# Norm entries of a two-layer-type transformer begun inside the program that feeds them; last chunks by token tile, scaled rows turned by the identity, GpSimd's first low halves

## The reference

```python
for l in range(2):                                  # first block
    h = rms_norm(x, attn_norm[l])
    x = x + mix(h @ w_in[l]) @ w_out[l]             # attentions and a gated scan in mix
    hf = rms_norm(x, ffn_norm[l]) @ w_up[l]
    x = x + (gelu(conv(gate(hf))) * val(hf)) @ w_down[l]          # w_down: 2816 x 1024
for l in range(2):                                  # second block
    y = mix2(x @ w_in_2[l])
    h = layer_norm(ALPHA * x + y @ w_out_2[l], ln1_g[l], ln1_b[l])
    x = layer_norm(ALPHA * h + peer_ffn(h, ...), ln2_g[l], ln2_b[l])
```

## Time and profile before

| | us |
|---|---|
| median of 3 runs | 2827.97 (2822.35 to 2829.43) |
| the profiled execution | 2826.24 |
| its span | 2824.5 |
| TensorE busy (matmuls) | 2651.6, 94% |
| VectorE, ScalarE, GpSimd busy | 2054.0, 1496.3, 176.2 |
| mean granted clock of TensorE | 0.979 |

### The profile page before, as it was taken

One profiled execution on the slowest core, in us unless ns is written; L12 is line 12 of the kernel. 1 busy time (PEld: TensorE's weight loads), 2 busy tenths in 40 slices (PEclk: granted clock), 3 DMA queues, 4 the chain that ended last, 5 costly groups with the idle time before them and its releaser, 6 DMA issues. The chain is left out here.

```text
span 2824.5 us, 56598 instructions
## 1 busy us (share of the span) xinstructions
PE 2651.6 (94%) x17272; PEld 2387.2 (85%) x17272; DVE 2054.0 (73%) x4610; ACT 1496.3 (53%) x2949; POOL 176.2 (6%) x136
## 2 busy tenths in 40 slices
PE   7989999989988899799999999988998999999997
PEld 6869988779977899799988888777998999888886
DVE  5767767767767668877767777787589777677777
ACT  5545556645555444466655555555454566555554
POOL 0000000000000044300000000000344000000000
PEclk9989999989999999999999999999999999999999
DMA  5225654236653477555567777625576555677775
GB/s 194 86 68 166 186 154 162 74 112 184 186 162 101 150 222 225 165 171 176 174 199 233 234 233 232 213 92 174 174 230 192 160 175 171 187 233 235 232 234 179
DMA packets 194306, 503.49 MB, mean 178 GB/s; under 512 B 22561, under 2 KB 88353, under 8 KB 192801
## 3 DMA queue, kind: packets, MB, share of 16 engines
q1 hardware_dynamic: 194208, 502.28, 56.8%
HBM read 467.59 MB, written 34.60 MB: 178 GB/s over the span
## 5 line engine op out<-in xcount | busy, mean ns | idle before, releaser
L182 DVE TENSOR_TENSOR w_lo<-w_raw,w_hi 128x512 fp32r<-128x512 f32 (+1 forms) x1464 | 994.8, 684 | 357.3 <-ACT w_hi L173 337.4
L173 ACT ACTIVATE w_hi<-w_raw 128x512 fp32r<-128x512 f32 (+2 forms) x1592 | 925.7, 621 | 203.4 <-PE banks_right L217 136.7
L215 PE MATMUL up_up<-hT_hi,w_hi 128*128 128x256 f32 x2048 | 595.8, 291 | 26.6 <-DVE w_lo L182 20.5
L217 PE MATMUL up_up<-hT_hi,w_lo 128*128 128x256 f32 x2048 | 582.6, 284 | 0.0
L216 PE MATMUL up_up<-hT_lo,w_hi 128*128 128x256 f32 x2048 | 582.3, 284 | 0.0
L215 PEld LDWEIGHTS up_up<-hT_hi,w_hi 128*128 128x128 f32 x2048 | 396.1, 193 | 31.2 <-DVE w_lo L182 23.9
L227 PE MATMUL banks_left<-w_hi,expert_hi 128*128 128x512 f32 x1024 | 408.1, 399 | 7.8 <-DVE w_lo L182 7.8
L228 PE MATMUL banks_left<-w_lo,expert_hi 128*128 128x512 f32 x1024 | 407.6, 398 | 0.0
L229 PE MATMUL banks_left<-w_hi,expert_lo 128*128 128x512 f32 x1024 | 407.4, 398 | 0.0
L216 PEld LDWEIGHTS up_up<-hT_lo,w_hi 128*128 128x128 f32 x2048 | 395.6, 193 | 0.0
L217 PEld LDWEIGHTS up_up<-hT_hi,w_lo 128*128 128x128 f32 x2048 | 395.0, 193 | 0.0
(11 more groups left out here) (374 smaller groups left out, 3863.6 us busy)
## 6 DMA issues: line engine op xcount, KB each, us to landing
w_raw<-in_peer_u_c SPq DMA_DIRECT2D x256, 512.0 KB, 3.5
w_raw<-in_peer_v SPq DMA_DIRECT2D x256, 512.0 KB, 3.6
w_raw<-in_w_up_c SPq DMA_DIRECT2D x88, 512.0 KB, 3.7
expert_gelu_held<-expert_gelu SPq DMA_DIRECT2D x256, 128.0 KB, 1.7
expert_back<-expert_gelu_held SPq DMA_DIRECT2D x256, 128.0 KB, 3.3
w_raw<-in_w_down SPq DMA_DIRECT2D x44, 512.0 KB, 4.1
w_raw<-in_w_in_r SPq DMA_DIRECT2D x40, 512.0 KB, 3.6
w_raw<-in_w_in_c SPq DMA_DIRECT2D x32, 512.0 KB, 4.0
```

The source lines that it names most:

```text
L173: self.nc.scalar.activation(self.w_hi[:, k % SLOTS, 0:width], self.raw_half(k, width), ACT.Copy).then_inc(self.sem("w_hi_done"), 1)
L182: self.nc.vector.tensor_tensor(self.w_lo[:, k % SLOTS, 0:width], self.raw_half(k, width), self.w_hi[:, k % SLOTS, 0:width].bitcast(F32), A ...
L215: self.nc.tensor.matmul(bank, hi, self.hT_hi[:, c, :], start=(c == 0), stop=False)
L217: last = self.nc.tensor.matmul(bank, lo, self.hT_hi[:, c, :], start=False, stop=(c == DC - 1))
```

## The change

It touches every entry, the end of every program that feeds one, and `finish`.

- The last chunk of an out-projection (the last two in `SecondMiddle` and `DownPhase`) goes by token tile first: `last_halves` finishes both banks of tile 0, then those of tile 1. It signals `acc_done` for the two banks of tile 0.
- The next entry exists before its block: in the feeding program VectorE adds three of the four quarters of the sum and, for a layer norm, takes their statistics and the scale of tile 0; ScalarE splits the first two weight halves, and squares tile 0 (RMS) or loads the square root's table and takes tile 0's root (layer norm).
- In the entry, RMS turns tile 0 by the diagonal matrix as before; tile 1 is scaled by rows, half on ScalarE, half on VectorE, and turned by the identity. A layer norm scales and shifts `x` in place and turns both tiles by the identity; `rows` then multiplies that by the gain.
- The first four low halves are made by GpSimd; high halves 2 and 3 stand between the copies of the chunks. TensorE waits for single chunks.
- In `finish` token tile 0 goes through GpSimd (times gain, plus bias, by halves), tile 1 through VectorE, and four stores of half the size go out.

```diff
+    def last_halves(self, pe, chunks, acc, done):
+        for t in range(TT):
+            cols = slice(t * P, (t + 1) * P)
+            for i, (k, act_hi, act_lo) in enumerate(chunks):
+                end = i == len(chunks) - 1
+                for h in range(2):
+                    if t == 0:
+                        pe.wait_ge(self.sem("w_lo_done"), k + h + 1)
+                    hi, lo = self.w_hi[:, (k + h) % SLOTS, :], self.w_lo[:, (k + h) % SLOTS, :]
+                    bank = acc[:, t, h, :]
+                    self.nc.tensor.matmul(bank, act_hi[:, cols], hi, start=False, stop=False)
+                    self.nc.tensor.matmul(bank, act_hi[:, cols], lo, start=False, stop=False)
+                    last = self.nc.tensor.matmul(bank, act_lo[:, cols], hi, start=False, stop=end)
+                    if t == TT - 1:
+                        last.then_inc(self.sem("w_used"), 1)
+                    elif end:
+                        last.then_inc(done, 1)
...
+    def arrived(self, dve, t, h):
+        if t == 0:
+            dve.wait_ge(self.acc_done, h + 1)
+        else:
+            dve.wait_ge(self.K.sem("w_used"), self.k0 - 1 + h)
+    def add_half(self, t, h):
+        x = self.x[:, t, h]
+        return self.K.nc.vector.tensor_tensor(x, x, self.add[:, t, h], ALU.add)
+    def early_vector(self, dve):
+        for t, h in ((0, 0), (0, 1), (1, 0)):
+            self.arrived(dve, t, h)
+            self.add_half(t, h).then_inc(self.added, 1)
+    def early_scalar(self, act, junk=None):
+        for h in range(2):
+            self.K.split_hi(act, self.k0 + h, self.width)
     def chunk_ready(self, pe, c):
-        if c % 2 == 0:
-            pe.wait_ge(self.lo_done, c // 2 + 1)
+        pe.wait_ge(self.lo_done, c + 1)
+    def pool(self, pool):
+        for h in range(EARLY):
+            self.K.split_lo_too(pool, self.k0 + h, self.width)
...
+class RmsEntry(TurnEntry):
+    def square(self, act, t, h, junk):
+        if self.add is not None:
+            act.wait_ge(self.added, 2 * t + h + 1)
+        self.K.nc.scalar.activation(junk, self.x[:, t, h], ACT.Square,
+                                    accum_out=self.K.ns[:, t, h:h + 1]).then_inc(self.squared, 1)
+    def sqrt(self, act, t):
+        act.wait_ge(self.squared, 2 * t + 2)
+        act.wait_ge(self.based, t + 1)
+        ns = self.K.ns[:, t]
+        self.K.nc.scalar.activation(ns[:, 3:4], ns[:, 1:2], ACT.Sqrt, scale=1.0 / D, bias=ns[:, 2:3]).then_inc(self.root, 1)
+    def base(self, dve, t):
+        dve.wait_ge(self.squared, 2 * t + 1)
+        ns = self.K.ns[:, t]
+        self.K.nc.vector.tensor_scalar(ns[:, 2:3], ns[:, 0:1], 1.0 / D, EPS1, ALU.mult, ALU.add).then_inc(self.based, 1)
+    def early_scalar(self, act, junk):
+        super().early_scalar(act)
+        for h in range(2):
+            self.square(act, 0, h, junk[:, h])
+    def tensor(self, pe):
+        pe.wait_ge(self.scaled, 1)
+        for c in range(DC):
+            self.K.nc.tensor.matmul(self.ps[:, c, 0:P], self.K.x[:, 0, c * P:(c + 1) * P], self.diag[:], start=True, stop=True)
+        for c in range(DC):
+            if c == 0:
+                pe.wait_ge(self.left_half, 1)
+            if c == DC // 2:
+                pe.wait_ge(self.right_half, 1)
+            self.turn(c, 1, self.rows)
+    def scalar(self, act):
+        K, A = self.K, self.K.nc.scalar
+        if self.add is None:
+            self.early_scalar(act, self.spare[:, 0])
+        self.sqrt(act, 0)
+        for h in range(2):
+            self.square(act, 1, h, self.spare[:, 0, h])
+        self.sqrt(act, 1)
+        act.wait_ge(self.scaled, 2)
+        A.activation(self.spare[:, 1, 0], self.x[:, 1, 0], ACT.Copy, scale=K.ns[:, 1, 4:5]).then_inc(self.left_half, 1)
+        K.split_hi(act, self.k0 + 2)
+        for j in range(DC // 2):
+            act.wait_ge(self.turned, j + 1)
+            for c in (2 * j, 2 * j + 1):
+                A.activation(K.hT_hi[:, c, :], self.ps[:, c, :], ACT.Copy, scale=self.gain[:, c:c + 1]).then_inc(self.hi_done, 1)
+            if j == 1:
+                K.split_hi(act, self.k0 + 3)
+    def vector(self, dve):
+        K, V = self.K, self.K.nc.vector
+        link = lambda ins: K.dve.link(dve, ins)
+        self.base(dve, 0)
+        if self.add is not None:
+            self.add_half(1, 1).then_inc(self.added, 1)
+        dve.wait_ge(self.root, 1)
+        link(V.reciprocal(K.ns[:, 0, 4:5], K.ns[:, 0, 3:4]))
+        V.tensor_scalar(self.diag[:], K.ident[:], K.ns[:, 0, 4:5], None, ALU.mult).then_inc(self.scaled, 1)
+        self.base(dve, 1)
+        dve.wait_ge(self.root, 2)
+        V.reciprocal(K.ns[:, 1, 4:5], K.ns[:, 1, 3:4]).then_inc(self.scaled, 1)
+        dve.wait_ge(self.scaled, 2)
+        V.tensor_scalar(self.spare[:, 1, 1], self.x[:, 1, 1], K.ns[:, 1, 4:5], None, ALU.mult).then_inc(self.right_half, 1)
+        for j in range(DC // 2):
+            dve.wait_ge(self.hi_done, 2 * j + 2)
+            for c in (2 * j, 2 * j + 1):
+                V.scalar_tensor_tensor(K.hT_lo[:, c, :], self.ps[:, c, :], self.gain[:, c:c + 1],
+                                       K.hT_hi[:, c, :].bitcast(F32), ALU.mult, ALU.subtract).then_inc(self.lo_done, 1)
...
+class LayerNormEntry(TurnEntry):
+    def norm_act(self, act, t, part):
+        act.wait_ge(self.ready, t + 1)
+        x, ns = self.K.x[:, t, part], self.K.ns[:, t]
+        self.K.nc.scalar.activation(x, x, ACT.Identity, scale=ns[:, 3:4], bias=ns[:, 4:5]).then_inc(self.rows_act, 1)
+    def early_vector(self, dve):
+        link = lambda ins: self.K.dve.link(dve, ins)
+        for h in range(2):
+            self.arrived(dve, 0, h)
+            link(self.add_half(0, h))
+            ins = self.stats(0, h)
+        link(ins)
+        self.variance(dve, 0)
+        self.arrived(dve, 1, 0)
+        link(self.add_half(1, 0))
+        self.K.dve.mark(self.stats(1, 0))
+        self.inverse(dve, 0)
+    def early_scalar(self, act, junk=None):
+        if self.gain is not None:
+            super().early_scalar(act)
+        self.K.nc.scalar.activation(self.K.ns[:, 0, 5:6], self.K.eps[:, 1:2], ACT.Sqrt)
+        self.sqrt(act, 0)
+    def last_stats(self, dve):
+        link = lambda ins: self.K.dve.link(dve, ins)
+        link(self.add_half(1, 1))
+        link(self.stats(1, 1))
+        self.variance(dve, 1)
+    def tensor(self, pe):
+        for t in range(TT):
+            for c in range(DC):
+                if c == 0:
+                    pe.wait_ge(self.rows_act, t + 1)
+                if t == 1 and c == DC // 2:
+                    pe.wait_ge(self.rows_dve, 1)
+                self.turn(c, t, self.K.x[:, t])
+    def scalar(self, act):
+        K, A = self.K, self.K.nc.scalar
+        self.norm_act(act, 0, slice(0, D))
+        self.sqrt(act, 1)
+        self.norm_act(act, 1, slice(0, D // 2))
+        for j in range(DC // 2):
+            two = slice(2 * j, 2 * j + 2)
             if j % 2 == 0:
                 act.wait_ge(self.turned, j + 1)
                 for c in (2 * j, 2 * j + 1):
                     A.activation(self.h[:, c, :], self.ps[:, c, :], ACT.Identity, scale=self.gain[:, c:c + 1],
                                  bias=self.bias[:, c:c + 1]).then_inc(self.shifted[0], 1)
             act.wait_ge(self.shifted[j % 2], 2 * (j // 2 + 1))
+            if j == 0:
+                for c in (0, 1):
+                    A.activation(K.hT_hi[:, c, :], self.h[:, c, :], ACT.Copy).then_inc(self.hi_done, 1)
+            else:
+                A.activation(K.hT_hi[:, two, :], self.h[:, two, :], ACT.Copy).then_inc(self.hi_done, 2)
+            if j < 2:
+                K.split_hi(act, self.k0 + 2 + j, self.width)
     def vector(self, dve):
         K, V = self.K, self.K.nc.vector
+        self.last_stats(dve)
+        self.inverse(dve, 1)
+        dve.wait_ge(self.ready, 2)
+        V.tensor_scalar(self.x[:, 1, 1], self.x[:, 1, 1], K.ns[:, 1, 3:4], K.ns[:, 1, 4:5], ALU.mult,
+                        ALU.add).then_inc(self.rows_dve, 1)
         def shift(j):
                 V.tensor_scalar(self.h[:, c, :], self.ps[:, c, :], self.gain[:, c:c + 1], self.bias[:, c:c + 1],
                                 ALU.mult, ALU.add).then_inc(self.shifted[1], 1)
+        def low(c, n):
+            dve.wait_ge(self.hi_done, c + n)
+            part = slice(c, c + n)
+            V.tensor_tensor(K.hT_lo[:, part, :], self.h[:, part, :], K.hT_hi[:, part, :].bitcast(F32),
+                            ALU.subtract).then_inc(self.lo_done, n)
+        shift(1)
+        low(0, 1)
+        low(1, 1)
+        low(2, 2)
+        shift(3)
+        low(4, 2)
+        low(6, 2)
...
+                if i == DC - 2 and h == 0:
+                    K.last_halves(pe, [(k0 + k + 2 * u, *self.out_parts(self.OUT_ORDER[i + u])) for u in range(2)],
+                                  acc, self.following.acc_done)
+                elif i < DC - 2:
...
     def tensor_tile(self, pe, j, n):
```

(17 more changed lines are left out.)

386 lines of the change are left out of this document (171 added, 215 removed).

## The result

The changed kernel took 2783.6 us in the median of 4 runs (2781.1 to 2789.9), the kernel before 2827.6 in 4 runs beside it: a ratio of 0.985 (95% interval 0.983 to 0.987), 44 us less. The forecast was 2817 and its range went down to 2808: the way was right, the size was not. The profiled span fell from 2824.5 to 2782.2 us, 42.3 us.

The account below looks back on a forecast made before the run. TensorE's work plus its waits was taken as the bound; 8.7 + 0.5 + 1.9 + 6.3 - 2.6 - 0.4 = 14.4 us, less 3.5 for the clock, gave 11: 2817 us, own range 2811 to 2822, wider 2808 to 2828.

Parts of the forecast that it names:

- the part on the bound: Opening step: TensorE, busy 94% of the span, bounds the kernel, with one chain of waits at each hand-over.
- 3.5 for the clock: Allowance for TensorE's clock falling to half at the norm hand-overs: 3.5 us lost, bounds 0 and 9.
- RMS entries: Three RMS norm entries with a sum: an earlier first tile gains 2.9 us each, 8.7 in all.
- First entry and turn: First RMS entry, with nothing to begin early, gains 0.5 us; the turn without a norm gains 1.9.
- Layer norms: Three layer-norm entries: first tile at E + 14.1 against 16.2 (E: last matmul's end), 2.1 us each, 6.3 in all.
- E + 14.5: Sign of error: a layer norm's first tile done later than 14.5 us after E, the last matmul's end.
- (a): Rival, nothing in the way: full clock, no turns with GpSimd; 18 us gained, 2810 us, chance 0.15.
- (b): Rival, given back: later waits absorb the entries' gain, half the 14 us or less, 2822 to 2828; 0.25 with (d).
- (c): Rival, colder and slower than before: clock at half in all seven hand-overs, 23 us cost, 2836 us, chance 0.10.
- The wait in `DownPhase`: One wait for tile 127's low halves before both last tiles costs 1.3 us in each DownPhase, 2.6 in all.
- The end: In finish, alternating VectorE and GpSimd gain 0.3 us, more clears cost 0.7: together -0.4, between -0.9 and +2.0.
- Rival (d): Early work does not start early, as VectorE or ScalarE are still busy: about 3 us gained, 2825; 0.25 with (b).

Follow-up runs that it names:

- e1: The kernel before with 160 bytes of unused SBUF allocated behind the epsilons and nothing else: 2804.6 us, ratio 0.992.
- e3: The kernel after the change with 32 unused bytes ahead of expert_hi and expert_lo alone: 2807.8 us, ratio 0.993.
- i1: The kernel after the change with DownPhase's last two tiles waited for separately and the RMS entries' root table loaded ahead of the squares: 2784.0 us.
- e5: The kernel after the change with nothing of a norm entry begun inside the program that feeds it: 2806.9 us, ratio 0.993.
- m1: A kernel of TensorE alone: 512-column fp32r products at varied starts of weights and moving rows, 227.0 to 234.3 ns from matmul to matmul.
- m2: As m1 with the moving rows fixed, only the weights' start moved, and the width varied: 113.3 to 120.1 ns at 256 columns.
- i3: i1's kernel with hT moved to start 64 bytes ahead of w_hi within 256 (192 unused bytes ahead, 64 behind): 2750.5 us, ratio 0.973.
- i4: i1's kernel with hT moved to start 64 bytes behind w_hi within 256 (64 unused bytes ahead, 192 behind): 2774.5 us, ratio 0.981.

## Why the prediction was wrong

**The step that failed** is the last sentence of the part on the bound: "Behind each first tile TensorE is the bound again, so I let a tile that is done earlier move all that follows", with a rate taken as fixed. The term for the steady loops was nothing, and the prediction gives no reason why their rate should stay. The change left the instructions of the down product's rounds as they were, but it moved their operands against each other: 234.3 ns from matmul to matmul became 226.7. e1 gives that part without the change and e3 takes it away from it, 23 to 24 us by the medians. Between the 11 us forecast and the 42.3 of the span lie 31.3: 22.8 in the two down products (-20.2 where +2.6 stood), 4.7 in the mixing programs, 1.1 in the feed-forward's outputs and 2.7 at the hand-overs (16.2 where 17.0 less 3.5 for the clock stood). The allocation of `ns` and `nstats` stood in the diff, and so did the two rates in the trace of before, 0.227 us in the out-projection and 0.234 in the down product. I used the first in the sum and did not ask why the second was longer. By the map the answer lay in the starts: `hT_hi` and `w_hi` are alike within 256 bytes, `expert_hi` and `w_hi` were 96 apart.

**RMS entries.** 8.7 us forecast, 8.3 measured, unevenly: 3.4 and 3.3 where I wrote 2.9, and 1.6 in the one between. There the table load stood where I had put it and TensorE turned 1.7 us sooner, as in the others, but the clock was at half:

```profile
400.94 1.28 ACT L392 ACT_TABLE_LOAD   x1 [0.92 <-DVE norm_scalars L398]
...
403.12 3.78 PE L408 MATMUL banks_right<-norm_scale,x 128*128 128x128 f32 x16 [3.20 <-DVE norm_scale L442]
```

The same sixteen rows took 2.05 us in the first feed-forward's entry, so the lower clock has the 1.7 us that are missing. i1 gains 1.5 us by moving the load of 1.28 away, and its sixteen rows took 3.42 us, partly at full clock. First entry and turn: 0.4 and 2.2 against 0.5 and 1.9.

**Layer norms.** 6.3 forecast and 4.7 measured. In the first one E is 899.28. Its low beside GpSimd took 1.35 us, where others took 0.69, as forecast, and the first product came at E + 8.3 instead of E + 12.2; but the first tile was done at E + 15.3, later than the E + 14.5 that I had named as a sign of error:

```profile
899.05 0.39 PE L255 MATMUL banks_right<-w_hi,hT_lo 128*128 128x512 f32 x1
...
907.59 0.55 PE L224 MATMUL banks_right<-hT_hi,w_hi 128*128 128x256 f32 x1 [0.83 <-DVE hT_lo L573]
...
908.43 1.35 DVE L573 TENSOR_TENSOR hT_lo<-ln_chunks,hT_hi 128x512 fp32r<-128x512 f32 x1 [0.66 <-ACT hT_hi L550]
...
914.55 0.63 ACT L182 ACTIVATE w_hi<-w_raw 128x512 fp32r<-128x512 f32 x1 [2.34 <-PE banks_right L226]
```

The 24 products took 7.0 us, before 4.0 (928.28 to 932.23). The stretches of 20 us, after and then before (busy share and count of each engine, then the granted clock):

```profile
903.00:923.00 20.00, 17.19 (x111) 16.03 (x110) 11.53 (x21) 10.91 (x20) 3.76 (x3) 0.74 0.62 213
```
```profile
915.00:935.00 20.00, 13.36 (x87) 12.27 (x86) 15.11 (x29) 11.10 (x19) 0.00 (x0) 0.83 0.41 160
```

A mean of 0.74 is 10.4 us at half clock (1.2 of 2.4 GHz), 0.83 is 6.8, and now they lie on the products, where before most fell on turning and waiting. That gives back 3.0 of the 3.9 us. So the clock cost about what I had feared in the first and last layer norm (1.1 and 1.0 us under the sum at full clock, 1.0 feared in each) and 1.7 in one RMS entry, and nothing to be seen in the others: hand-overs and waits together came to -13.9 us, between the 14.4 at full clock and the forecast's 11. The 4.5 us that the prediction names for the clock are 5.0 by its own figures (three layer norms at 1.0, four RMS entries at 0.5).

**The rivals (a) to (c).** (a), nothing in the way, is refuted as a mechanism, by the clock of 0.5 and the low of 1.35 us; its 18 us are 4 above the 13.9, and its 1.7 for the end should have been 2.6 by the prediction's own E + 8.8. (b), given back, does not hold: all 16.2 us are still there at a matmul well behind the first tiles, and the mixing programs behind them got no longer but by 0.2 us in one. (c) is refuted: no hand-over got slower. The turn's stretch held no time at half clock in any of the 14 kernels, with sixteen turns between its products.

**The wait in `DownPhase`** was 1.13 us twice (1.3 forecast), the release as computed. That the pair need not wait as one (i1) gives back 0.5, not all.

**The end.** 0.74 us shorter, where 0.4 longer was forecast. The clears were last and are longer as forecast (47 in 3.3 us, before 36 in 2.5), but the work ahead of them ended at E + 9.7 (E = 2767.70) and not at E + 11.4: the four operations of VectorE took 1.5 to 1.75 us each beside GpSimd's of 1.3 to 1.7, largely at the same time and not in strict turns. The last of each:

```profile
2775.29 1.59 POOL L3158 TENSOR_TENSOR x<-x,w_raw 128x512 f32<-128x512 f32 x1
2775.68 1.75 DVE L3176 SCALAR_TENSOR_TENSOR x<-x,norm_scalars,w_raw 128x512 f32<-128x512 f32 x1
```

**The mixing programs.** -4.7 us, of which 3.4 in one: it had 13.7 us at half clock before and 3.4 after. No term of the forecast spoke of the clock outside the hand-overs. That gain need not be the change's: the same program took 104.9 us with 3.4 at half clock in e2 too, which is the kernel before with 32 unused bytes.

**Rival (d):** e5 shows the contrary of (d): the early work began early, and 23 us hang on it. That is more than the 16 that the hand-overs gained, since without the early start the new order is worse than the old one in the layer norms and at the end.

## What to carry on

Before you take a steady loop as fixed, list which buffers the diff moves; a cadence that shifts by some ns with equal waits is the sign. Compare the start-to-start time of equal matmuls between phases: a difference within one trace may be a gain that lies open. Hold the starts of weights and moving rows at a distance chosen by a measured map (here: alike for 512 columns, the weights 64 bytes past the moving rows for 256), and test a change of order against a baseline with the same placement.

## What was unexpected of the hardware

With nothing else at work, fp32r products of 512 columns took 227.0 to 234.3 ns by the difference of the two SBUF starts modulo 256 bytes (m1). Of 256 columns they took 113.3 to 120.1 as the weights' start moved (m2); that the difference counts there too is borne out by i3 and i4, which moved the other operand. 128 columns took 111.7 at every start. At a difference of 64 the 256-column product has two steady rhythms, 113.3 and 117.7 ns, in one kernel and phase; what picks one was not found. The mechanism was not found either: only the map is shown, and only for the order of this kernel's triples.
